# Compression tiles stored by token phase, and the first merge gate products placed between the query turns

## The reference, cut to what matters

```python
CMP_BLOCK, CMP_STRIDE, CMP_HIDDEN, HEAD_DIM = 32, 16, 128, 64
def compress(k, pos_emb, w1, b1, w2):          # k: (1, 512, 2 groups, 64)
    n_cmp = (S - CMP_BLOCK) // CMP_STRIDE + 1  # 31
    idx = np.arange(n_cmp)[:, None] * CMP_STRIDE + np.arange(CMP_BLOCK)[None, :]
    blk = k[:, idx] + pos_emb[None, None, :, None, :]
    flat = jnp.moveaxis(blk, 3, 2).reshape(B, n_cmp, N_KV_GROUPS, CMP_BLOCK * HEAD_DIM)
    hid = jax.nn.gelu(flat @ w1 + b1)          # (.., 2048) @ (2048, 128)
    return hid @ w2
...
k_cmp = compress(k_c, ...); v_cmp = compress(v_c, ...)
```

## Time and profile before

| what | us |
|---|---|
| median of 3 runs | 1343.82 |
| lowest and highest | 1342.89, 1344.29 |
| span of the profiled execution | 1344.7 |
| PE busy in it | 1314.8 |
| DVE busy in it | 884.6 |
| ACT busy in it | 365.6 |
| POOL busy in it | 270.1 |

### The profile page before, as it was taken

One profiled execution on the slowest core, in us unless ns is written; L12 is line 12 of the kernel. 1 busy time (PEld: TensorE's weight loads), 2 busy tenths in 40 slices (PEclk: granted clock), 3 DMA queues, 4 the chain that ended last, 5 costly groups with the idle time before them and its releaser, 6 DMA issues.

```text
span 1344.7 us, 16228 instructions
## 1 busy us (share of the span) xinstructions
PE 1314.8 (98%) x5728; PEld 883.8 (66%) x5728; DVE 884.6 (66%) x2049; ACT 365.6 (27%) x900; POOL 270.1 (20%) x264
## 2 busy tenths in 40 slices
PE   4999999999999999999999999999999999999998
PEld 3544455544544545886455556888788888888887
DVE  5888999679431555564455676676676777777564
ACT  4223121225200102223455676110133233330000
POOL 1168578215003387700000000001000000000000
PEclk9899999999999999999999999999999999999999
DMA  9773524651312112302102002112212313224210
GB/s 320 180 153 100 157 42 143 198 184 36 121 38 77 63 63 63 125 32 94 63 1 64 1 1 61 66 63 89 84 63 82 107 63 125 64 68 167 77 58 32
DMA packets 89996, 120.59 MB, mean 90 GB/s; under 512 B 15448, under 2 KB 51614, under 8 KB 89916
## 3 DMA queue, kind: packets, MB, share of 16 engines
q1 hardware_dynamic: 85216, 110.81, 26.6%
q10 hardware_dynamic: 2956, 5.05, 1.2%
q0 software_dynamic: 1744, 3.70, 1.0%
HBM read 111.00 MB, written 6.84 MB: 88 GB/s over the span
## 4 chain that ended last, share of the span: by engine, by line
PE 94%; DVE 3%; ACT 1%; issue 1%; DMA 1%; ACTq 0%; POOL 0%; DVEq 0%; POOLq 0%
PE bank L1502 18%; PE bank L872 12%; PE bank L1528 10%; PE bank L885 9%; PE bank L1429 7%; PE bank L1387 6%; PE bank L907 5%; PE bank L1160 4%; PE bank L1270 4%; PE bank L1341 3%; PE bank L1367 3%; PE bank L936 2%; PE bank L1472 2%; PE bank L1205 2%; PE bank L1043 1%
## 5 line engine op out<-in xcount | busy, mean ns | idle before, releaser
L1502 PE MATMUL bank<-arena 128*128 128x256 f32 x1120 | 242.0, 379 | 0.0
L1502 PEld LDWEIGHTS bank<-arena 128*128 128x128 f32 x1120 | 212.7, 190 | 29.3 <-issue 0.4
L872 PE MATMUL bank<-arena 128*128 128x512 f32 (+1 forms) x384 | 157.0, 565 | 0.0
L1528 PE MATMUL bank<-arena 128*128 128x256 f32 x616 | 133.1, 379 | 0.0
L885 PE MATMUL bank<-arena 128*128 128x512 f32 x288 | 127.7, 596 | 0.0
L1528 PEld LDWEIGHTS bank<-arena 128*128 128x128 f32 x616 | 117.0, 190 | 15.9
L907 PEld LDWEIGHTS bank<-arena 128*128 128x128 f32 (+2 forms) x660 | 78.4, 144 | 72.3 <-issue 41.9
L872 PEld LDWEIGHTS bank<-arena 128*128 128x128 f32 x384 | 71.9, 190 | 77.8 <-issue 73.6
L907 PE MATMUL bank<-arena 128*128 128x128 f32 (+2 forms) x660 | 94.0, 280 | 20.4 <-ACT arena L1612 7.1
L2913 DVE CUSTOM_DVE_ANT_0 arena<-bank,arena 128x128 f32<-128x128 f32 (+3 forms) x128 | 57.8, 489 | 73.1 <-PE bank L1341 72.3
L1429 PE MATMUL bank<-arena 128*128 128x256 f32 x448 | 97.6, 379 | 0.0
(11 more groups left out here) (387 smaller groups left out, 1951.6 us busy)
## 6 DMA issues: line engine op xcount, KB each, us to landing
arena<-in_w_in SPq DMA_DIRECT2D x14, 2048.0 KB, 7.8
arena<-in_w_up SPq DMA_DIRECT2D x20, 1024.0 KB, 6.6
arena<-in_w_ada SPq DMA_DIRECT2D x16, 512.0 KB, 8.9
arena<-in_w_down SPq DMA_DIRECT2D x8, 1024.0 KB, 7.3
arena<-in_w_out SPq DMA_DIRECT2D x2, 2048.0 KB, 9.3
arena<-in_w_attn_br SPq DMA_DIRECT2D x8, 512.0 KB, 7.3
arena<-in_w_o SPq DMA_DIRECT2D x2, 2048.0 KB, 7.6
rb_dram<-rb_one_dram ACTq DMA_DIRECT2D x1, 2560.0 KB
```

The costliest lines, as they stand in the source:

```text
L872: mm = pe.matmul(ps[:, 0:n], act[:, k, 128 * t:128 * t + 128], w[:, k, 0:n], start=(k == 0), stop=(k == kt - 1))
L1502: mm = pe.matmul(ps, left[:, k, :], right[:, k, :], start=(first and k == 0), stop=(k == 3), skip_group_check=True)
L1528: mm = pe.matmul(down_acc(i, name), left, right, start=first and name in ("P1", "P7", "P2", "P4"), stop=last, skip_group_check=True)
```

## The change

`kcT` is stored by phase: token n = 16 c + r stands at r x 32 + c, so that the tokens of one phase r of sixteen lie side by side. The products read 31 neighbouring columns of each of the three planes where they read every sixteenth. ACT's copies now read their PSUM banks at a step of 16 and write side by side; the upper half, which is one token ahead, takes two copies (480 columns and 31 columns) where it took one, and the position plane takes two copies of 16 columns where it took one of 32. The memset of the position plane on POOL covers the same words. On PE, P1 and P2 of the first merge gate pair stand ahead of the last four query turns, where they stood behind them; the wait for the rotation of the second half of the queries (`qrope_done`) moves with the turns.

```diff
-        kcT = arena[:, OB0 - 4096:OB0 - 4096 + 3072].rearrange("p (a g n) -> p a g n", a=2, g=3)
+        kcT = arena[:, OB0 - 4096:OB0 - 4096 + 3072].rearrange("p (a g r c) -> p a g r c", a=2, g=3, r=16)
...
                     mm = pe.matmul(ps[:, 0:3 * NCMP], w[:, 16 * a + k, :],
-                                   kcT[:, a, :, 2 * k:2 * k + 16 * (NCMP - 1) + 1:16],
+                                   kcT[:, a, :, 2 * k % 16, 2 * k // 16:2 * k // 16 + NCMP],
                                    start=(k == 0), stop=(k == 15))
...
                 turn(("qt2", m), [row2[:, t, 128 * m:128 * m + 128] for t in range(TT)])
-            pe.wait_ge(qrope_done, 2 * TT)
-            for m in range(4):
-                turn(("qt2", 4 + m), [q2b[:, t, 128 * m:128 * m + 128] for t in range(TT)])
...
             h_products(0, "P1", "P2")
+            pe.wait_ge(qrope_done, 2 * TT)
+            for m in range(4):
+                turn(("qt2", 4 + m), [q2b[:, t, 128 * m:128 * m + 128] for t in range(TT)])
             h_products(1, "P1", "P2")
...
-            act.activation(kcT[:, :, 2, 0:32:2], abank("pos")[:, 0:32].rearrange("p (a b) -> p a b", a=2), ACT.Copy)\
-               .then_inc(afree("pos"), 1)
+            for a in range(2):
+                ins = act.activation(kcT[:, a, 2, 0:16:2, 0:2],
+                                     abank("pos")[:, 16 * a:16 * a + 16].rearrange("p (c r) -> p r c", c=2), ACT.Copy)
+            ins.then_inc(afree("pos"), 1)
             many_columns_in("ks", ksT, range(4))
             for n in range(4):
                 aux_ready(act, ("kc", n))
-                act.activation(kcT[0:64, n // 2, n % 2, :], abank(("kc", n))[0:64, :], ACT.Copy)
-                act.activation(kcT[64:128, n // 2, n % 2, 0:S - 1], abank(("kc", n))[64:128, 1:S], ACT.Copy)\
-                   .then_inc(afree(("kc", n)), 1)
+                dst, src = kcT[:, n // 2, n % 2, :, :], abank(("kc", n))[:, :].rearrange("p (c r) -> p r c", r=16)
+                act.activation(dst[0:64, :, :], src[0:64, :, :], ACT.Copy)
+                act.activation(dst[64:128, 15:16, 0:31], src[64:128, 0:1, 1:32], ACT.Copy)
+                act.activation(dst[64:128, 0:15, :], src[64:128, 1:16, :], ACT.Copy).then_inc(afree(("kc", n)), 1)
...
-            pool.memset(kcT[:, :, 2, :], 0.0).then_inc(kc_zero, 1)
+            pool.memset(kcT[:, :, 2, :, :], 0.0).then_inc(kc_zero, 1)
```

## The result

The changed kernel is slower: 1346.32 us (median of 20 runs, 1343.76 to 1349.19) against 1343.36 us (20 runs, 1341.57 to 1346.95) before, ratio 1.002 with a 95% interval of 1.0012 to 1.0027. The prediction was no change, 1343.8, with "slower by over 0.2%" at 9%. The median lies inside the stated range (1341.6 to 1346.9), but the kernel before turned out at 1343.36, and the loss is clear: 2.96 us between the medians, 2.7 us by the ratio (1.6 to 3.6), where the sum had 0. One execution of the kernel before, beside the later runs, took 5097.27 us and is left out of their comparison.

The account below looks back on a forecast made before the run. PE, busy 98% of the span, was taken as the bound, except before the fourth query turn, where a DMA and DVE's sums set the pace; 3.3 us gained and 3.3 us new idle time sum to 0: 1343.8 us, range 1341.6 to 1346.9.

Parts of the forecast that it names:

- no change: Whole kernel: no net change, with or without faster products, 1343.8 us; chance 0.58.
- slower by over 0.2%: Whole kernel: more than 2.7 us slower than 1343.8, outside the band taken as same; chance 0.09.
- The packed products: PE's 64 compression records: 0.108 us each with neighbouring columns instead of 0.160, a gain of 3.3 us.
- Who takes the gain back: PE before the fourth query turn: still waits for DVE until 549.29, idle 4.14 us for 0.84; 3.3 us lost again.
- The reordering: PE behind the fourth turn: same instructions in another order, 0.9 us left before P5 would wait; cost 0.
- ACT's copies: ACT's strided and extra small copies from PSUM: 0.8 us more for the banks, done before the products; cost 0.
- The clock: PE around the fourth turn: clock falls in the idle time, 1.7 us lost (0.23) or 3.0 or more (0.09).
- the rarer case: Long clock fall, at least 6 us, around the fourth turn: 1346.8 us or more; chance 0.09.
- The baseline: Whole kernel: forecast starts from the median, 1343.8 us; the profiled span, 1344.7, is 0.9 us above it.
- The wait was where the chain puts it: Rival denied here: the fourth turn's releaser moves with the products, so all 3.3 us are gained, 1340.5; chance 0.10.
- The products did not stay at 0.160 us: Rival denied here: weight loads set the compression products' pace, no time moves, 1343.8; within the 0.58 for no net change.

Follow-up runs that it names:

- run with the order alone: Old storage, only P1 and P2 of the first pair moved between the query turns, against the kernel before: 1343.99 us against 1343.76, ratio 1.0003.
- packed-only run: Storage by phase with PE's list in the old order, against the kernel before: 1346.36 us against 1343.76, ratio 1.0014.
- run with two products: Changed kernel plus two extra products of 256 columns between third and fourth turn, against the kernel before: 1344.00 us against 1344.09, ratio 0.9999.

## Why the prediction was wrong, point by point

**The packed products: right.** 64 records in 7.12 us, 0.111 each, for 0.108 forecast and 0.160 before; the gain is 3.1 us, for 3.3. The Trainium skill's rule ("SBUF — State Buffer", "Door 1: The DMA port swizzle"), that each step onto a new short line of SBUF costs extra, agrees with these runs: 0.160 us with a line for every column, 0.111 with columns side by side.

**Who takes the gain back: right.** The DMA took 7.63 us for 7.50, the four sums 540.14 to 544.11, 3.97 us for 4.11, and the fourth turn came 12.37 us behind `("up", 3)`, for 12.4. Idle time 3.96 us, for 4.14.

**The reordering: right in its cost of 0.** The margin at P5 was larger than forecast. DVE's sum that frees bank 1 ran from 554.45 and took 0.42 us, so it ended at 554.9, and P5 follows the first 16 of the 56 products that begin at 553.10, at about 556.6: 1.7 us left, for 0.9. The run with the order alone shows 0.

**ACT's copies: right.** At a step of 16 the 64x512 copy takes 0.59 us, as L1867 did without one, and the small copies 0.19 us:

```profile
517.52 0.59 ACT L1869 ACTIVATE arena<-bank 64x512 f32<-64x512 f32 x1
518.12 0.19 ACT L1870 ACTIVATE arena<-bank 64x31 f32<-64x31 f32 x1
518.21 0.55 ACT L1871 ACTIVATE arena<-bank 64x480 f32<-64x480 f32 x1
...
522.04 0.56 ACT L1871 ACTIVATE arena<-bank 64x480 f32<-64x480 f32 x1
```

ACT was done at 522.6, the products began at 532.22.

**The clock: the step that failed, twice.** The sum had "gain on the products 3.3, new idle time 3.3, sum 0" and no term for the clock; the term measured 2.46 us. First the choice. The prediction saw the mechanism, its place and the idle time of 4 us, and gave it 32% against 58% for no change. What it held against it, the 35 transposes in a row and the slow products, were stretches in which PE had work, and say nothing of one in which it stands still. What it held for it, that no gap of 4 us occurs in the rest of the trace, is true only behind the first 18 us, and there it means that the trace could not speak against the fall. The two longer gaps of before stand at its start:

```profile
8.18 0.42 PE L907 MATMUL bank<-arena 32*128 32x32 f32 x2 [4.82 <-DMA arena<-in_a_im]
...
17.83 6.12 PE L907 MATMUL bank<-arena 128*128 128x128 f32 x32 [7.10 <-ACT arena L1612]
```

The granted clock reads 1.00 in both, but the 32 transposes behind the second took 0.191 us each, where 20 took 0.120 each at 1.00 and 0.227 in the packed-only run at 0.50. Why they were slow is not shown; these gaps are at any rate no evidence that the clock holds. Then the size. The low stretch was taken as 3.4 us, all of it under work, for 1.7 us, from the first fall in the earlier trace rows. It lasted about 6.8 us in the changed kernel (543.0 to 549.8), of which 1.8 lay in the idle time, and cost 2.5 us; in the two other profiled executions with 3.94 us of idle time it was about as long (542.8 to 549.6, and 545.0 to 551.8). That is the length of the longer fall of before, which the prediction had made the rarer case at 9% and priced at 3.0 us or a little more. The ends of that fall, beside the earlier trace rows:

```profile
60.00:61.00 1.00, 1.00 (x2) 0.67 0.00 0
...
67.00:68.00 1.00, 1.00 (x4) 0.91 0.00 0
```

They give (1 - 0.67) / 0.5 + 6 + (1 - 0.91) / 0.5 = 6.8 us.

The Trainium skill's rule ("TensorE: Matmul & The Clock Gate", "HAM oscillation — how this bites in real kernels"), a wait between bursts drops the clock and the burst behind it starts cold, is what happened in all three profiled executions with 3.94 or 3.96 us of idle time. The 3.09 us of the run with two products did not drop it in the profiled execution. The prediction quoted the rule as speaking against this change and weighed it too low.

**The baseline.** The prediction set the span of before, 1344.7 us, 0.9 us above the median. The profiles of after show the device time of an execution 1.9 us above its span (1344.58 for 1342.7), so the profiled execution of before took, by an estimate from these two, some 1346.6 us, well above the median, with both early falls in it. The median as the base of the forecast was right none the less (1343.82 then, 1343.36 over 20 executions).

**The other rivals.** The wait was where the chain puts it. The products did not stay at 0.160 us.

## What to carry to other kernels

A shorter product in front of a wait that another engine ends is worth nothing, and where it makes an idle gap longer it can cost: before shortening work on the bounding engine, ask what that engine will wait for next, and put real work into that gap or end the wait first. Here the engine that held the bank (DVE) had the release behind four sums that PE did not need yet. Moving two instructions ahead of them turned a loss of 2.5 us into a gain of 4.2 in the stretch, and putting P1 and P2 one turn earlier into a gain of 3.5; the packed products paid only with one of the two. When a clock fall is a rival, look for a gap of that length in the trace; if there is none, the trace is silent, and that is no evidence for the clock holding.

## What the runs showed of the hardware

- Idle times of 0.84, 2.22 and 3.09 us ahead of the same turn left the granted clock at 1.00 in the profiled executions; 3.94 and 3.96 us brought it to 0.50 in all three, 2.2 to 2.3 us after PE had stopped. It then stayed there for about 6.8 us although PE had work again for the last 5.0 to 5.2 us of them, products of 256 columns in two of the three and mostly transposes in the third.
- A float32 product of 93 columns with 128 x 128 weights takes 0.111 us per record with columns side by side and 0.160 us with columns 64 bytes apart.
- Transposes of 128 x 128 follow the granted clock: 20 took 2.40 us at 1.00 and 4.53 us at 0.50.
- ACT reads 64 x 512 values from PSUM at a step of 16 values in 0.59 us, as fast as side by side (0.59 us before).
